# Two transformer blocks on one core: the norm after the hybrid mixer in the early form, the fourth weight tile's split moved ahead, and a later wait for the recurrent mixer's masks

## The reference, cut to what matters

```
def modulate(t, sub):
    return rms_norm(t, norm_g[layer, sub]) * (1.0 + mod[:, sub, 1]) + mod[:, sub, 0]
h = modulate(x, 1)
y = hybrid_mixer(h, ...)                       # layer 0; mlstm_block in layer 1
x = x + (1.0 + mod[:, 1, 2]) * y
h = modulate(x, 2)
x = x + 0.5 * (1.0 + mod[:, 2, 2]) * swiglu(h, ...)
```

## Time and profile before

| | |
|---|---|
| median of 3 runs | 3580.46 us (3576.4 to 3591.96) |
| the profiled execution's own time | 3580.06 us |
| its span, first to last instruction | 3578.2 us |
| TensorE busy, share of the span | 96% |
| VectorE, ScalarE, GpSimd busy | 56%, 34%, 10% |
| mean granted TensorE clock | 0.983 |

### The profile page before, as it was taken

How to read it: one execution, slowest core, us unless ns; L and a number is a source line. 1 busy time by engine, 2 the same in 40 slices (tenths; PEclk the granted TensorE clock), 3 DMA queues, 4 the chain that set the end, 5 groups by cost and what they waited for, 6 DMA issues and landing times. The chain is left out here.

```text
span 3578.2 us, 56582 instructions
## 1 busy us (share of the span) xinstructions
PE 3448.2 (96%) x22456; PEld 2780.9 (78%) x22456; DVE 2018.7 (56%) x2820; ACT 1212.7 (34%) x1783; POOL 360.7 (10%) x264
## 2 busy tenths in 40 slices
PE   7999999999999999999999999999988999999998
PEld 5888777878888788876678888877757787878886
DVE  6666666846665666575443433365666773464343
ACT  3222346432222322243343322233434543233231
POOL 1000003410000000000101000130103330010000
PEclk9999999999999999999999999999979999989999
DMA  6554321125553455421032222222210002223232
GB/s 246 197 193 169 125 76 71 55 93 188 188 207 139 179 191 203 156 86 54 1 112 88 96 97 106 84 88 83 63 33 6 8 6 73 95 65 100 89 99 71
DMA packets 103765, 382.75 MB, mean 107 GB/s; under 512 B 11424, under 2 KB 15136, under 8 KB 103200
## 3 DMA queue, kind: packets, MB, share of 16 engines
q1 hardware_dynamic: 103584, 380.15, 30.7%
HBM read 378.01 MB, written 2.10 MB: 106 GB/s over the span
## 5 line engine op out<-in xcount | busy, mean ns | idle before, releaser
L457 PE MATMUL bank<-h_hi,w_hi 128*128 128x512 f32 x2576 | 1015.5, 394 | 29.2 <-DVE w_lo L252 26.5
L459 PE MATMUL bank<-h_hi,w_lo 128*128 128x512 f32 x2576 | 1005.6, 390 | 0.0
L458 PE MATMUL bank<-h_lo,w_hi 128*128 128x512 f32 x2576 | 1005.3, 390 | 0.0
L252 DVE TENSOR_TENSOR w_lo<-w_raw,w_hi 128x1024 fp32r<-128x1024 f32 (+2 forms) x480 | 634.3, 1321 | 397.7 <-ACT w_hi L246 386.5
L246 ACT ACTIVATE w_hi<-w_raw 128x1024 fp32r<-128x1024 f32 (+2 forms) x475 | 521.1, 1097 | 299.8 <-PE bank L459 260.4
L457 PEld LDWEIGHTS bank<-h_hi,w_hi 128*128 128x128 f32 x2576 | 485.3, 188 | 146.5 <-DVE w_lo L252 30.0
L459 PEld LDWEIGHTS bank<-h_hi,w_lo 128*128 128x128 f32 x2576 | 485.0, 188 | 102.4
L458 PEld LDWEIGHTS bank<-h_lo,w_hi 128*128 128x128 f32 x2576 | 485.5, 188 | 100.7 <-issue 1.9
L457 PE MATMUL bank<-f_gu_hi,w_hi 128*128 128x512 f32 x704 | 278.5, 396 | 0.0
L458 PE MATMUL bank<-f_gu_lo,w_hi 128*128 128x512 f32 x704 | 278.2, 395 | 0.0
L459 PE MATMUL bank<-f_gu_hi,w_lo 128*128 128x512 f32 x704 | 278.2, 395 | 0.0
(11 more groups left out here) (645 smaller groups left out, 4759.4 us busy)
## 6 DMA issues: line engine op xcount, KB each, us to landing
ada_tiles<-in_ada SPq DMA_DIRECT2D x180, 512.0 KB, 4.3
w_raw<-in_gu SPq DMA_DIRECT2D x176, 512.0 KB, 4.4
w_raw<-in_dn SPq DMA_DIRECT2D x64, 704.0 KB, 5.0
w_raw<-in_w_ff SPq DMA_DIRECT2D x64, 512.0 KB, 3.5
w_raw<-in_w_hyb SPq DMA_DIRECT2D x36, 512.0 KB, 3.4
w_raw<-in_w_rkv SPq DMA_DIRECT2D x24, 512.0 KB, 3.5
w_raw<-in_w_attn SPq DMA_DIRECT2D x20, 512.0 KB, 3.5
w_raw<-in_w_hout SPq DMA_DIRECT2D x16, 512.0 KB, 3.4
```

The lines of the kernel that those rows point to most:

```text
L252: K.nc.vector.tensor_tensor(K.w_lo[:, half, 0:kb * P], K.w_raw[:, slot, 0:kb * P], K.w_hi[:, half, 0:kb * P].bitcast(F32), ALU.subtract).t ...
L457: nc.tensor.matmul(K.ps[bank][:], wh, hi, start=start, stop=False)
L458: nc.tensor.matmul(K.ps[bank][:], wh, lo, start=False, stop=False)
L459: last_mm = nc.tensor.matmul(K.ps[bank][:], wl, hi, start=False, stop=stop)
```

## The change

Four edits:

- `gemm`: in the early form, tile 3 is split (`split_hi`, `split_lo`) in the step of t = 0, ahead of the evacuation of tile 0, and no longer in the step of t = 1. It holds in all early heads.
- `hybrid` gets `follow`, the head of f01, which is now an early one. VectorE makes the gain at the start of the `w_hout` product; each evacuation of it gets one more operation on ScalarE and one on VectorE.
- The high and low parts that `ahead_act` and `ahead_dve` write now have names of their own (`ahead_hi`, `ahead_lo`). By default these are `K.h_hi` and `K.h_lo`; in the hybrid mixer, whose last product still reads those, they lie in its arena.
- `rwkv`: the waits of VectorE, GpSimd and TensorE for the masks at the start are gone; TensorE waits for them in `key_squares(0)`.

```diff
                     if head and isinstance(i, int) and t < 3:
-                        if t < 2 and not (early and t == 0):
+                        if early and t == 0:
+                            split_hi(K, act, kb, 3 % RING, 1, g0 + 3)
+                        elif t < 2 and not early:
                             split_hi(K, act, kb, (t + 2) % RING, t % SPLIT, g0 + t + 2)
...
-                        if t < 2 and not (early and t == 0):
+                        if early and t == 0:
+                            split_lo(K, dve, kb, 3 % RING, 1, g0 + 3)
+                        elif t < 2 and not early:
                             split_lo(K, dve, kb, (t + 2) % RING, t % SPLIT, g0 + t + 2)
...
-                    hi, lo, bank, start, stop = mm(c, 0)
+                    _, _, bank, start, stop = mm(c, 0)
+                    hi, lo = head.ahead_hi[:, c, :], head.ahead_lo[:, c, :]
...
-def hybrid(K, nxt, head, gate):
+def hybrid(K, nxt, head, gate, follow):
...
+    follow.ahead_hi = K.at("hyb_ahead_hi", [P, DC, S], F32R, A + GATE * CH)
+    follow.ahead_lo = K.at("hyb_ahead_lo", [P, DC, S], F32R, A + Z * CH)
...
             act.wait_ge(free.sem, free(o + 1))
+            act.wait_ge(K.x_written.sem, K.x_written(follow.GAIN_STEPS))
             squares.by_act(act, K.x[:, o:o + 1, :], o, o % 2)
+            follow.ahead_act(act, o)
...
             v.scalar_tensor_tensor(x, K.ps[HOUT_BANK[o]][:], K.coef[:, o:o + 1], x, ALU.mult, ALU.add).then_inc(free.sem, 1)
+            follow.ahead_dve(dve, o)
...
         dve.wait_ge(K.coef_done.sem, K.coef_done(1))
+        follow.gain_ahead(dve)
...
             dve.wait_ge(ka_done, 3)
-            dve.wait_ge(loaded, 16)
-
-        @block.gpsimd
-        def _(pool):
-            pool.wait_ge(loaded, 16)
-
-        @block.tensor
-        def _(pe):
-            pe.wait_ge(loaded, 16)
...
             def key_squares(i, x):
+                if i == 0:
+                    pe.wait_ge(loaded, 16)
                 after(pe, i, "sq", 1)
...
-            elif step != "hyb":
+            else:
                 follow = Modulated(K, *terms(K, *places[plan[n + 1]]), early=True)
```

More of the change, by code:

```diff
@@ L704, in __init__ @@
         self.gain, self.scale, self.shift, self.early = gain, scale, shift, early
+        self.ahead_hi, self.ahead_lo = K.h_hi, K.h_lo
     def gain_ahead(self, dve):
@@ L715, in ahead_act @@
         K = self.K
-        K.nc.scalar.activation(K.h_hi[:, bass.ds(o, 1), :], K.x[:, bass.ds(o, 1), :], ACT.Identity, scale=K.gain[:, bass.ds(o, 1)]).then_inc(K.h_hi_done.sem, 1)
+        K.nc.scalar.activation(self.ahead_hi[:, bass.ds(o, 1), :], K.x[:, bass.ds(o, 1), :], ACT.Identity, scale=K.gain[:, bass.ds(o, 1)]).then_inc(K.h_hi_done.sem, 1)
     def ahead_dve(self, dve, o):
@@ L720, in ahead_dve @@
         dve.wait_ge(K.h_hi_done.sem, K.h_hi_done(o + 1))
-        K.nc.vector.scalar_tensor_tensor(K.h_lo[:, bass.ds(o, 1), :], K.x[:, bass.ds(o, 1), :], K.gain[:, bass.ds(o, 1)],
-                                         K.h_hi[:, bass.ds(o, 1), :].bitcast(F32), ALU.mult, ALU.subtract).then_inc(K.h_ready.sem, 1)
+        K.nc.vector.scalar_tensor_tensor(self.ahead_lo[:, bass.ds(o, 1), :], K.x[:, bass.ds(o, 1), :], K.gain[:, bass.ds(o, 1)],
+                                         self.ahead_hi[:, bass.ds(o, 1), :].bitcast(F32), ALU.mult, ALU.subtract).then_inc(K.h_ready.sem, 1)
     def ahead_advance(self):
@@ L1871, in coefficients @@
         dve.wait_ge(K.coef_done.sem, K.coef_done(1))
+        follow.gain_ahead(dve)
     gemm(K, d["w_hout"], DC, 2 * DC, nxt, out_mm, out_wait, out_act, out_dve, turn=2 * DC, squares=squares, dve_first=coefficients,
          pe_more=out_pe, pool_work=out_pool, dve_lead=lambda dve, t: None if t else state_dve(dve, DC - 1))
+    follow.ahead_advance()
     free.base += DC
@@ L3740, in build @@
                 with stage(K):
-                    hybrid(K, nxt, head, gate)
+                    hybrid(K, nxt, head, gate, follow)
             elif step == "ml":
```

## The result

| | before | changed |
|---|---|---|
| median, 16 runs each | 3584.22 us | 3597.13 us |
| all runs | 3576.40 to 3593.84 | 3592.44 to 3607.19 |
| span of the profiled execution | 3578.2 us | 3605.4 us |
| its mean granted clock | 0.983 | 0.978 |

The ratio is 1.0037, with a 95% interval of 1.0027 to 1.0046: 13 us slower, which is real and lies within the 0.5% that were called no change. The forecast of 3595 is 2 us away, and 3597.13 is in the range.

What follows compares the result with a forecast made beforehand. TensorE, busy 96% of the span, was taken as the bound, so only its gaps count. Terms 8.9 + 0.9 - 2.6 = +7.2, plus 8.4 for the clock, gave +15.6 on 3580.06: 3595 us, range 3578 to 3602.

Steps and rivals of the forecast that it cites:

- Edit 1, VectorE's queue: Five already early heads: VectorE idles before tile 3's low part, tile 4 starts later; +8.9 us, plus 3.07 in f01.
- The clock: TensorE's merged long wait before tile 4 lowers the granted clock in f10, f01, hyb and ml: 2.1 us each, +8.4.
- the row of passes: Profile row after a 4.5 us wait: nine passes take 3.9 us instead of 2.05; with two more, 2.2 us lost.
- the 6.6 us: Time at half clock around that profiled wait, 2.2 + 4.4; by the skill's rule 3.3 us per place.
- the rival of a clock that stays up: At the long waits before tile 4 the clock does not fall: 3580 + 7, so 3587 us; chance 25%.
- Edit 2: f01's head made early: -2.2 us at tile 4, together +0.9 with the moved split's 3.07; added `w_hout` operations cost 0.
- Edit 3: Mixer's start, mask waits moved to `key_squares(0)`: reciprocal and all later work earlier, -2.6 us, bounds -2.0 and -3.5.
- The sum: Whole kernel: +7.2 us without the clock and +8.4 from the clock, +15.6 on 3580.06.
- plain gain: Rival: VectorE is still busy when tile 3's high part is ready, so nothing is pushed back: -9.4, 3571 us; chance 9%.
- The case of five falls: Rival: the clock falls in all five long-wait heads and b2 pays its 1.1: +19.3, 3599 us; chance 15%.
- an early head that isn't covered: Rival: f01's added operations aren't hidden in the `w_hout` product and its early tile wins nothing: +20, 3600 us; chance 8%.

Runs made afterwards that it cites:

- (3): The changed kernel with only VectorE's low part of tile 3 put back behind tile 0's evacuation, ScalarE's high part left ahead: 3590.59 us, 1.0008 of the kernel before.
- (8): The changed kernel with only ScalarE's high part of tile 3 put back behind tile 0's evacuation, VectorE's low part left ahead: 3601.00 us, 1.0042 of the kernel before.
- experiment 7: The kernel before with only f01's head made early, including the added operations in the `w_hout` product: 3580.11 us, 0.9983 of the kernel before.
- kernel 1: The changed kernel with tile 3's split put back behind tile 0's evacuation on both engines, all else kept: 3576.57 us, 0.9974 of the kernel before.
- kernels 2 and 5: First: the kernel before with only tile 3's split moved ahead, 1.0045. Second: the changed kernel with filler products in TensorE's long waits at four heads, 1.0027.

## Why the prediction was right

**Edit 1, VectorE's queue: right, with one half missed.** The idle time was forecast at 1.9 and measured at 1.86 in hyb and f01, 1.85 in f10 and ml. Tile 4's shift, as the distance from the low parts of tiles 1 and 2 to tile 4, was forecast and measured at 1.90 and 1.95 in hyb, 1.94 and 1.94 in ml, 3.07 and 3.6 in f10, and 0 and 0.0 in f11. In f10 the modulation load does end last, as the prediction put it:

```profile
1198.78 1.23 DVE L252 TENSOR_TENSOR w_lo<-w_raw,w_hi 128x1024 fp32r<-128x1024 f32 x1 [1.85 <-ACT w_hi L246]
...
1208.53 1.54 DVE L556 SCALAR_TENSOR_TENSOR ada_acc<-ada_tiles,c_turn,ada_acc 128x512 f32<-128x512 f32 x2 [2.27 <-DMA ada_tiles<-in_ada]
1209.98 1.22 DVE L252 TENSOR_TENSOR w_lo<-w_raw,w_hi 128x1024 fp32r<-128x1024 f32 x1
```

The idle time for this load is 2.27 where it was 0.63. b2 was forecast at 1.97 and measured at 0.84, and its wait at 3.4 and measured at 2.07. That term was mis-sized: VectorE was idle as forecast (1.92). But from the first evacuation to tile 4's low part it then took 6.6 us, and before 8.9 less the one low part of 1.1 between them, 7.8. VectorE's timeline in b2's head, of the changed kernel:

```profile
2393.11 1.23 DVE L252 TENSOR_TENSOR w_lo<-w_raw,w_hi 128x1024 fp32r<-128x1024 f32 x1 [1.92 <-ACT w_hi L246]
...
2394.39 1.63 DVE L2637 TENSOR_TENSOR lora<-shift_raw 128x512 f32<-128x512 f32 x1
...
2400.97 1.21 DVE L252 TENSOR_TENSOR w_lo<-w_raw,w_hi 128x1024 fp32r<-128x1024 f32 x1
```

and of the kernel before:

```profile
2358.33 1.64 DVE L2624 TENSOR_TENSOR lora<-shift_raw 128x512 f32<-128x512 f32 x1
...
2367.23 1.21 DVE L252 TENSOR_TENSOR w_lo<-w_raw,w_hi 128x1024 fp32r<-128x1024 f32 x1
```

The same operations of VectorE vary in length beside GpSimd's (0.68 or 1.7 us for one), and here they met otherwise; that reading wasn't tried by an experiment. The prediction looked for that effect only on the costly side. What it left out altogether is that ScalarE's half is harmful by itself (3); it changed no term, as VectorE's half hides it (8).

**The clock: right in places and sum.** Forecast was a fall in f10, f01, hyb and ml, at 2.1 each, 8.4; measured a fall at those four, 8.9, as 3.1, 2.6, 1.6 and 1.6. The Trainium skill ("TensorE: Matmul & The Clock Gate", Terms), which counts the time at the reduced clock times one half, gave an estimate of 13.2; the measured 8.9 is nearer the row of passes. Most of that distance is the 6.6 us that the prediction took for every place. In the changed kernel's trace the granted clock is 0.84 over 441 to 452, 0.72 over 828 to 840, 0.72 over 1207 to 1219 and 0.83 over 1585 to 1595; that is 20.4 us at half clock, and from these the rule's estimate is 10.2. What is left is time in which TensorE was idle. In hyb and ml the clock was at half for some 3.5 us each and not for 6.6, so there the price is below 2.1. One reading of the rows was wrong: 0.92 over 5 us, from 2653 on, means that the clock fell after 4.2 us and not after 4.6. That made the rival of a clock that stays up look likelier than the row had it, and changed no term.

**Edit 2: its sign as forecast, its size open.** f01's tile 0 follows one pass behind the mixer's last, and the product's time is unchanged:

```profile
799.38 0.39 PE L464 MATMUL bank<-hyb_hi,w_lo 128*128 128x512 f32 x1
799.61 0.39 PE L417 MATMUL bank<-hyb_ahead_hi,w_hi 128*128 128x512 f32 x1
```

The prediction had -2.2; the ledger has -1.5 and -1.7 (7, 1), part of it scatter. The prediction's account misses a thing that the trace before shows: in the plain head the clock was already at half, and ten passes of tiles 0 and 1 followed each other at 0.43 us, which costs 2.0 us. In experiment 7 it stays at full speed through the early head. First before, then experiment 7:

```profile
798.00:802.00 4.00, 2.64 (x6) 2.16 (x7) 4.00 (x7) 3.51 (x6) 0.00 (x0) 0.50 0.00 0
...
795.00:830.00 35.00, 31.53 (x151) 25.13 (x150) 29.09 (x42) 15.42 (x23) 0.00 (x0) 1.00 0.38 135
```

So all of edit 2's gain may be this clock, and not a shorter path. With edit 1's cost there, +5.2 measured and 5.2 forecast (3.07 + 2.1), f01 stands at +3.5.

**Edit 3: right.** -2.6 forecast, -2.7 or -2.8 in nine traces. The first products start right behind the barrier:

```profile
2692.08 1.19 PE L3120 MATMUL bank<-lora,rw_w_lora 64*128 64x512 f32 x1 [5.38 <-PEq L103]
...
2695.38 1.87 PE L3130 MATMUL bank<-rw_masks,rw_a_dec 128*128 128x2 f32 x8 [1.22 <-DMA rw_masks<-in_rwkv_masks]
```

**The sum.** Forecast +15.6, measured by place +14.6 and by the medians +12.9. That 3595 came within 2 us of 3597.13 is in part luck: the sum was 2.7 too high, and the 3580 that it was added to is 4 below the median of the sixteen runs of before. Inside the sum b2's 1.1 too much stands against 0.5 too little in f10 and 0.5 in the clock. The rival "plain gain" (3571) fell on the idle time of 1.86 us, which it wanted below 1; "the clock stays up" (3587) fell on the clock of 0.50 to 0.63 behind four waits. The case of five falls (3599) fell in b2, and that of an early head that isn't covered (3600) on the `w_hout` product, which took as long as before.

## What to carry to other kernels

Before an instruction is moved ahead in an engine's stream, compare the time at which its input is ready with the time at which the engine comes to it: an idle time there is paid once by everything queued behind it, and again by whatever those results release (here a load). By the ledger, moving the split that was ready gained 7 us, and moving the one that wasn't lost 19. Two short waits of TensorE, merged into one, cost more than their sum as soon as the clock falls in them. And where executions scatter by more than the effect, subtract the traces place by place: medians gave 13 us with a cause nowhere in sight, the ledger gave each head its own number. Trace a kernel twice before a small one is trusted: here the same kernel came back within 0.3 us, but untouched heads of other kernels moved by up to 1.5.

## What the runs showed of the hardware

The clock's fall isn't a function of the wait's length alone. The same wait of TensorE in b2's head left the clock up in the changed kernel (2.07 us, 1.00 behind it) and brought it down in kernels 2 and 5 (2.10 us each, 0.57 and 0.79). A wait of 1.85 us in f01 was followed by 0.57 in kernel 3; waits of 1.84 in kernel 1 and 1.96 in kernel 7 at the same place were followed by 1.00. In ml the clock fell some 0.9 us after the wait had ended. And in the changed kernel a wait of 1.65 us behind hyb's head was followed by seven passes 0.43 us apart, which other executions don't have. Stretches of it, that wait with what follows:

```profile
552.40:557.40 5.00, 3.67 (x19) 2.94 (x17) 4.62 (x15) 1.65 (x3) 0.00 (x0) 1.00 0.01 3
557.40:562.40 5.00, 4.68 (x14) 3.69 (x15) 4.89 (x8) 2.38 (x4) 0.00 (x0) 0.66 0.35 105
```

The largest scatter is in ml's core. The changed kernel there:

```profile
1696.00:1814.00 118.00, 115.30 (x491) 77.51 (x490) 44.19 (x106) 32.62 (x72) 16.49 (x21) 0.89 0.00 1
```

It is the same 491 products as in the kernel before, 11 us longer in one execution than in another. What decides which execution gets it wasn't tried.
